# Expert blocks: activation in three parts, end by a count, and another order of the weights' high and low parts

## The reference, cut to what matters

```python
for e in range(N_EXPERTS):
    a = jax.nn.silu(hf @ w_e_gate[e]) * (hf @ w_e_up[e])
    y = y + combine[:, e:e + 1] * (a @ w_e_down[e])
```

## Time and profile before

| what | value |
|---|---|
| median of 3 runs | 1394.6 us |
| profiled execution | 1396.6 us |
| its span, first to last instruction | 1394.8 us |
| TensorE matmuls busy | 1316.3 us (94%) |
| VectorE busy | 779.7 us (56%) |
| ScalarE busy | 555.1 us (40%) |
| GpSimd busy | 318.5 us (23%) |
| expert stage on TensorE | 838.8 to 1323.2 us |
| mean granted TensorE clock | 0.990 of full speed |

### The profile page before, as it was taken

The page is one execution under the profiler, slowest core; times in us unless marked ns, Lnnn a source line. Parts: engine busy times, 40 slices in busy tenths (PEclk is TensorE's granted clock), DMA queues, the critical chain, the costliest instruction groups (busy, mean ns, idle before and its releaser), DMA issues.

```text
span 1394.8 us, 19837 instructions
## 1 busy us (share of the span) xinstructions
PE 1316.3 (94%) x7309; PEld 1017.4 (73%) x7310; DVE 779.7 (56%) x1014; ACT 555.1 (40%) x734; POOL 318.5 (23%) x449
## 2 busy tenths in 40 slices
PE   4999999999999999999999989999999999999984
PEld 2666678998787666666778777887777888887752
DVE  5734222324402267666799864558887242458648
ACT  0432022322212255555412143457776242457522
POOL 0133210003100257666166510000000000000053
PEclk9999999999999999999999999999999999999997
DMA  9854320102211342110433359669999151649764
GB/s 334 312 182 124 121 68 1 62 1 76 68 46 42 86 160 62 31 42 21 181 103 102 136 200 394 236 240 350 385 391 363 67 219 60 241 173 379 268 231 168
DMA packets 138776, 234.54 MB, mean 168 GB/s; under 512 B 57328, under 2 KB 58936, under 8 KB 138712
## 3 DMA queue, kind: packets, MB, share of 16 engines
q1 hardware_dynamic: 128440, 196.41, 39.9%
q0 software_dynamic: 6496, 23.60, 4.9%
q10 hardware_dynamic: 3776, 13.67, 2.4%
HBM read 197.96 MB, written 35.68 MB: 168 GB/s over the span
## 4 chain that ended last, share of the span: by engine, by line
PE 70%; POOL 7%; issue 6%; DVE 6%; ACT 5%; DMA 3%; SPq 1%; ACTq 1%; POOLq 0%; DVEq 0%
PE psum L831 65%; POOL arena L2098 5%; ACT high L1519 2%; DMA arena<-in_w_ada_mix 2%; PE psum L1243 1%; PE psum L1058 1%; DVE arena L2037 1%; DVE arena L2036 1%; PE psum L938 1%; ACT a_high L1551 1%; DVE arena L2029 1%; PE psum L1249 1%; DVE arena L2028 1%; PE psum L882 1%; PE psum L1152 0%
## 5 line engine op out<-in xcount | busy, mean ns | idle before, releaser
L831 PE MATMUL psum<-arena 128*64 128x128 f32 (+8 forms) x1396 | 165.9, 368 | 24.0 <-DMA arena<-in_w_ada_mix 15.1
L831 PE MATMUL psum<-win_high,x_low 128*128 128x512 f32 (+1 forms) x432 | 168.5, 390 | 0.0
L831 PE MATMUL psum<-high,h_high 128*128 128x512 f32 x416 | 163.8, 394 | 2.5 <-DVE h_low L1984 2.5
L831 PE MATMUL psum<-win_high,x_high 128*128 128x512 f32 (+1 forms) x416 | 166.2, 399 | 0.0
L831 PE MATMUL psum<-win_low,x_high 128*128 128x512 f32 (+1 forms) x416 | 162.3, 390 | 0.0
L831 PE MATMUL psum<-high,h_low 128*128 128x512 f32 x416 | 162.2, 390 | 0.0
L831 PEld LDWEIGHTS psum<-arena 128*64 128x64 f32 (+4 forms) x1396 | 83.2, 143 | 100.6 <-issue 72.7
L1840 DVE TENSOR_TENSOR_SCAN arena<-arena,psum 128x512 f32<-128x512 f32 (+3 forms) x112 | 108.2, 1003 | 19.8 <-ACT arena L1475 19.5
L1979 DVE TENSOR_TENSOR low_odd<-raw_odd,high 128x2048 fp32r<-128x2048 f32 x48 | 107.8, 2288 | 14.0 <-ACT high L1519 14.0
L1979 DVE TENSOR_TENSOR low_even<-raw_even,high 128x2048 fp32r<-128x2048 f32 x48 | 107.7, 2287 | 10.9 <-ACT high L1519 10.8
L2155 POOL COPY smalls<-smalls 128x1 int32 x26 | 4.8, 183 | 417.6 <-PE psum L1243 412.8
(11 more groups left out here) (260 smaller groups left out, 2417.2 us busy)
## 6 DMA issues: line engine op xcount, KB each, us to landing
raw_even<-in_w_e_gate SPq DMA_DIRECT2D x8, 2048.0 KB, 10.9
raw_even<-in_w_e_up SPq DMA_DIRECT2D x8, 2048.0 KB, 16.8
raw_even<-in_w_e_down SPq DMA_DIRECT2D x8, 2048.0 KB, 14.7
raw_odd<-in_w_e_gate SPq DMA_DIRECT2D x8, 2048.0 KB, 10.2
raw_odd<-in_w_e_up SPq DMA_DIRECT2D x8, 2048.0 KB, 16.4
raw_odd<-in_w_e_down SPq DMA_DIRECT2D x8, 2048.0 KB, 15.0
win<-in_w_in SPq DMA_DIRECT2D x7, 2048.0 KB, 7.9
expert_rows<-arena ACTq DMA_DIRECT2D x26, 512.0 KB, 6.5
```

Of the source, the lines that this page charges most:

```text
L831: pe_last[0] = nc.tensor.matmul(*x, **y)
```

## The change

The activation goes in three parts of 1, 1 and 2 turns of 128 columns, in PSUM banks 6, 7 and 0. The 64x64 turn and `s_edone` are gone: who waited for it waits for the count of finished down products (`s_yp`) against a number from `table`. A sigmoid of one column stands behind the router's exponentials. In an expert's last block ScalarE makes high chunks 0 and 1 after its sigmoid and 2 and 3 later; VectorE makes low chunk 4 behind the loop and low chunk 5 in the first block of the expert itself, after sigmoid times gate.

```diff
+        act_parts = ((0, 1, 6), (1, 2, 7), (2, 4, 0))
+        N_ACT = len(act_parts)
-        an = view(r_b + 17408, 2, 256)
+        an = view(r_b + 17408, 512)
...
-                            sp.wait_ge(s_edone, 2 * ee + k - 1)
+                            sp.wait_ge(s_yp, end)
...
-            sp.wait_ge(s_edone, EXPERTS - 1)
+            end = sp.value_load(table[0:1, EXPERTS - 1:EXPERTS], min_val=1, max_val=MAX_BLOCKS - 1)
+            sp.wait_ge(s_yp, end)
...
-                        for half in range(2):
-                            pe.wait_ge(s_a, 2 * b + half + 1)
-                            for f in range(2):
-                                last = nc.tensor.transpose(bank(6 + half)[:, f * P:(f + 1) * P],
-                                                           an[:, half, f * P:(f + 1) * P], ident)
+                        for i, (f0, f1, at) in enumerate(act_parts):
+                            pe.wait_ge(s_a, N_ACT * b + i + 1)
+                            for f in range(f0, f1):
+                                last = nc.tensor.transpose(bank(at)[:, (f - f0) * P:(f - f0 + 1) * P],
+                                                           an[:, f * P:(f + 1) * P], ident)
                             last.then_inc(s_at, 1)
...
-                            if f % 2 == 0:
-                                pe.wait_ge(s_aH, 2 * b + f // 2 + 1)
+                            part = [i for i, (f0, f1, _) in enumerate(act_parts) if f0 == f]
+                            if part:
+                                pe.wait_ge(s_aH, N_ACT * b + part[0] + 1)
...
-                    nc.tensor.transpose(bank(7)[0:64, 0:64], ident[0:64, 0:64], ident[0:64, 0:64]).then_inc(s_edone, 1)
...
             A(dd, dd, ACT.Exp).then_inc(s_rt2, 1)
+            A(table_warm, mhalf[:, 0:1], ACT.Sigmoid)
...
-                                high_parts(nxt, (0,), loads)
-                        for half in range(2):
-                            act.wait_ge(s_at, 2 * b + half + 1)
-                            A(a_high[:, 2 * half:2 * half + 2], bank(6 + half)[:, 0:256].rearrange(
-                                "p (f q) -> p f q", f=2), ACT.Copy).then_inc(s_aH, 1)
+                                high_parts(nxt, (0, 1), loads)
+                        for i, (f0, f1, at) in enumerate(act_parts):
+                            act.wait_ge(s_at, N_ACT * b + i + 1)
+                            A(a_high[:, f0:f1], bank(at)[:, 0:(f1 - f0) * P].rearrange(
+                                "p (f q) -> p f q", q=P), ACT.Copy).then_inc(s_aH, 1)
...
-                                high_parts(nxt, (1, 2, 3), loads)
+                                high_parts(nxt, (2, 3), loads)
...
-            act.wait_ge(s_edone, EXPERTS)
...
-            low_parts(0, (3, 4, 5), 0)
+            low_parts(0, (3, 4), 0)
...
-                        TT(an.rearrange("p a c -> p (a c)"), sg, bank(0), ALU.mult).then_inc(s_g1, 1)
+                        TT(an, sg, bank(0), ALU.mult).then_inc(s_g1, 1)
+                        with dve.If(b == first):
+                            low_parts(k, (5,), before - 6)
...
-                        for half in range(2):
-                            TT(an[:, half], an[:, half], bank(1)[:, half * 256:half * 256 + 256], ALU.mult).then_inc(s_a, 1)
+                        for f0, f1, _ in act_parts:
+                            fs = slice(f0 * P, f1 * P)
+                            TT(an[:, fs], an[:, fs], bank(1)[:, fs], ALU.mult).then_inc(s_a, 1)
...
-                        low_parts(nxt, (4, 5), before)
+                        low_parts(nxt, (4,), before)
...
-            pool.wait_ge(s_edone, EXPERTS)
+            pool.wait_ge(s_yp, total)
```

More of the change, by code:

```diff
@@ L340, in stream_step @@
         s_e = [[sem(f"expert_{w}_in{i}") for w in ("gate", "up", "down")] for i in range(2)]
-        s_edone = sem("expert_done")
         s_idx, s_hg, s_htr, s_hL = sem("index_ready"), sem("rows_gathered"), sem("rows_turned2"), sem("block_h_low")
@@ L618, in stream_step @@
         idc = rtiny(1, dt=I32)
+        table_warm = rtiny(1)
         def turned_weights(s):
@@ L1260, in _ @@
                                 mm(psum[2][:, hh, :], a_high[:, f, :], low_w[k][2][:, f, cols], start=False, stop=False)
-                            if f % 2 == 0:
-                                pe.wait_ge(s_aL, 2 * b + f // 2 + 1)
+                            if part:
+                                pe.wait_ge(s_aL, N_ACT * b + part[0] + 1)
                             for hh in range(2):
@@ L2001, in dve_pair @@
                         dve.wait_ge(s_gu, 2 * b + 2)
-                        for half in range(2):
-                            TT(an[:, half], an[:, half], bank(1)[:, half * 256:half * 256 + 256], ALU.mult).then_inc(s_a, 1)
[L2004 to L2007, removed]
+                        for f0, f1, _ in act_parts:
+                            fs = slice(f0 * P, f1 * P)
+                            TT(an[:, fs], an[:, fs], bank(1)[:, fs], ALU.mult).then_inc(s_a, 1)
+                        for i, (f0, f1, at) in enumerate(act_parts):
+                            dve.wait_ge(s_aH, N_ACT * b + i + 1)
+                            TT(a_low[:, f0:f1], bank(at)[:, 0:(f1 - f0) * P].rearrange(
+                                "p (f q) -> p f q", q=P), a_high_f[:, f0:f1], ALU.subtract).then_inc(s_aL, 1)
                         dve.wait_ge(s_hH, b + 2)
```

## The result

The changed kernel takes 1384.3 us (median of 4 runs, 1380.3 to 1389.3), the kernel before 1395.4 in the same comparison: a ratio of 0.9923, with a 95% interval of 0.9894 to 0.9951. Run again beside parts of the change it gave 0.9876 (0.9847 to 0.9904; 1378.5 us), and a third time 0.9891 (0.9871 to 0.9912; 1379.6 us). The forecast was 1380.8 us within 1378.0 to 1386.5.

The account below looks back on a forecast made before the run. TensorE was taken as the bound in the expert stage, so gains lie where it stands still: 5.5 + 6.0 + 2.3 = 13.8 us off the median of 1394.6 gives 1380.8 us. Range 1378.0 to 1386.5; the forecast alone, 1378.0 to 1383.5.

Parts of the forecast that it names:

- rival (a): In crowded blocks transfers become the bound, 18.7 us a block against a period of 18.02; 3 us lost, 1383.8; chance 0.11.
- Activation in three parts: Before the down products in 26 blocks: one turn less and a 128-column copy save 0.21 each, 5.5 us.
- End by a count: At 15 expert switches: dropping the 64x64 turn saves 0.40 each, 6.0 us.
- the sequencer's lead of 2.5 us: At the last expert's new block TensorE's sequencer was 2.5 us ahead, so the switch's 0.40 was given to the turn.
- rival (b): At expert switches the 0.40 belongs to the loop, not the turn: 6.0 us less gain, 1386.8; chance 0.08.
- Order and table: In nine crowded blocks: reordered high and low parts and the early sigmoid table remove 2.3 of 3.1 us of TensorE's wait.
- 0.40 late: In crowded blocks VectorE's product starts 0.40 after the up result (16.97 against 16.57), where 0.31 is allowed.
- the 0.8 of loss: Wait expected to remain in the nine crowded blocks, 0.09 each, because VectorE's product with the up result is late.
- the 13.0: In crowded blocks gate weights are used some 13.0 us after issue and land 10.8 after it.
- (c): Table loads stay in the loop: 1.28 in each of four crowded blocks, 5.1 us less gain, 1385.9; chance 0.07.
- (d): VectorE is the bound in crowded blocks, two more instructions adding 0.16 each: 1.5 us less gain, 1382.3; chance 0.04.
- (e): Slower: high parts before ScalarE's activation copies wait for late gate weights, 2.9 in nine blocks, 26 us, 1406.9; chance 0.03.

## Why the prediction was right

The forecast held: 1384.3, 1378.5 and 1379.6 us against 1380.8, all in the range and clearly faster. The first of them lies above the 1383.5 that the forecast alone allowed and next to rival (a)'s 1383.8; it is the trace that tells the two apart. By its own terms, which measure 5.7 + 6.0 + 3.2 = 14.9 against the stage's 14.6:

- **Activation in three parts, 5.5.** 0.22 in each of 26 blocks, 5.7. The copy of 128 columns takes 0.28 as the row of another line showed, and one turn less stands before it. With that the copy is through just as TensorE ends its last turn, so by this chain an even earlier copy would give nothing (not tried).
- **End by a count, 6.0.** 0.40 at 15 switches. The share between loop and turn was decided by the sequencer's lead of 2.5 us, and rightly: rival (b) falls with the run without a turn (no gap) and the one with a larger turn (0.12).
- **Order and table, 2.3 of 3.1.** All of the 3.2 went. The step that failed is the product with the up result "0.40 late": it came 0.26 late, within the 0.31 that the prediction left, because ScalarE's sigmoid starts 11.25 after the first down product (965.50 to 976.75) and not 11.33, VectorE's product with it 0.61 after that and not 0.63, and the up products end at 16.61 and not 16.57. The spacings of VectorE's parts are those of the forecast (0.61, 2.20 and 2.20). So the 0.8 of loss was not there.

What the prediction did not say is that these terms are no sum. It worked each out as if the others were there, which is right for the whole and wrong for a part. In the crowded blocks of the old order the activation hangs on a ring: ScalarE's copies of it, the next rows' high part, three high parts of weights, the copy of the result, two more high parts, then over the sigmoid and VectorE's low parts and products the turns, and ScalarE's copies again. The down products and the switch are not in it, since ScalarE comes to the copy of the result after they are done; a shorter switch or a smaller first part only makes TensorE arrive sooner and wait longer. The new order has two high parts and not three before the copy of the result, so that ScalarE waits for the down products (kernel before, then after):

```profile
968.88 1.03 ACT L1560 ACTIVATE arena<-psum 128x1024 f32<-128x1024 f32 x1
```

```profile
971.34 1.03 ACT L1563 ACTIVATE arena<-psum 128x1024 f32<-128x1024 f32 x1 [0.77 <-PE psum L834]
```

That opens the ring, and lets the other two terms count in nine more blocks: order and table give 2.7 without them, and with them the order alone 6.8 and the table alone 5.4. These two do not add up either, as one part missing is enough to make the crowded blocks late. Which half of the order does it, ScalarE's or VectorE's, was not tried apart.

The rivals. (a) The transfers did not become the bound: at the new period of 18.05 the engines moved 399 GB/s with a share of 1.04, where 393 at 1.03 had looked like full, and gate weights landed 11.1 us after issue and not 10.8, within the 13.0. The reading "393 is what they can do" was the error of that rival. (c) The loads went; its price of 5.1 measured 5.4 when they were put back. The rule of the Trainium skill on "per block" placement ("ScalarE activation tables: per-element evaluation and per-set limits", "Table sets in the compiler and the runtime") did not show in this form: one load in one place of the loop, gone once the table was loaded before it. (d) VectorE is busy 17.81 of 19.0 in such a stretch; TensorE's waits for it, up to 0.2 at the later turns, make no first down product later. (e) ScalarE had 2.19 us free before the activation copies.

The first median lay 3.5 us over the forecast. That part goes with the clock: the stage had its 14.6, less 1.6 on the first block in each of three profiled executions, and the execution of the first profile lost 4.1 before the stage. Of the fifteen runs of the changed kernel the four at a mean clock of 0.986 took 1384.6 us in the median, the three at 0.990 1379.6 and the three at 0.992 1376.7; the first comparison's four lay at 0.984 to 0.989, those of the second at 0.986 to 0.993. Whether the change has a share in the lower clock on the first block stays open: it fell there in all three profiles of the changed kernel, in one with its old order, and in one of the kernel before with a larger turn, and in neither of the two of the kernel before itself. It goes with the long stretch near 797 us: of the traces with TensorE's wait before the first block unfilled, four of the five with that stretch have it, and one of the six without. The prediction's lower bound, 1378.0, is 0.3 below what its own terms give (1394.6 - 15.8 - 0.5 = 1378.3); nothing hangs on that.

## What to carry to other kernels

Where one engine carries the end, list the places where it stands still by what it waits for, and ask of each whether the chain that ends the wait passes through the work that you mean to shorten: if not, the time won comes back as a longer wait, and an edit whose median shows nothing alone (here 1.0000, with 2.3 us in the stage) can be worth several us once that chain is free. An instruction that only raises a semaphore is not free on the engine that is the bound; count something that it does anyway. Price a table load by whether the engine is ahead or behind at that place: the same 1.28 us cost nothing in eight blocks and 1.4 in four.

## What was not expected of the hardware

A 64x64 turn between 128x128 work costs 0.40 us, a 128x128 one in its place 0.12. DMA engines that show a share of 1.03 at 393 GB/s still took blocks 5% closer together (399 at 1.04, and 414 in the second block's stretch).

```profile
855.75:873.81 18.06, 17.97 (x86) 14.79 (x85) 5.92 (x9) 6.90 (x8) 1.15 (x2) 1.00 1.03 414
```

And 2.5 us of idle TensorE between its turns and the first gate product was followed by 3.4 us at 1.2 GHz, which cost 1.4 to 1.6 us, in five of eleven executions (all three of the changed kernel) and not in the other six; with matmuls in that gap the two profiles taken show none. So the idle time alone does not bring the lower level on, and that the matmuls keep it away is not shown.
